# 28 identity matmuls on TensorE ahead of the transposes behind a double norm

## The reference

```python
# end of the first block, last layer
x = layer_norm(ALPHA * x + 0.5 * swiglu(x, ffn_w_gu[l, 1], ffn_w_down[l, 1]), ln_g[l, 2], ln_b[l, 2])
...
# start of the second block
h = rms_norm(x, norm1_g[l])
z = h @ w_in[l]
```

## Time and profile before

| | us |
|---|---|
| median of 3 runs | 1911.38 |
| lowest and highest run | 1909.96, 1911.92 |
| the profiled execution's own time | 1909.5 |
| its span, first to last instruction | 1907.7 |
| TensorE busy in it | 1878.9 |
| VectorE busy | 1259.6 |
| ScalarE busy | 968.5 |
| TensorE waiting between 950 and 1000 us | 5.0 |

### The profile page before, as it was taken

The page is one execution under the profiler, slowest core; times in us unless marked ns, Lnnn a source line. Parts: engine busy times, 40 slices in busy tenths (PEclk is TensorE's granted clock), DMA queues, the critical chain, the costliest instruction groups (busy, mean ns, idle before and its releaser), DMA issues.

```text
span 1907.7 us, 26911 instructions
## 1 busy us (share of the span) xinstructions
PE 1878.9 (98%) x10465; PEld 1633.4 (86%) x10465; DVE 1259.6 (66%) x1598; ACT 968.5 (51%) x1242; POOL 35.8 (2%) x67
## 2 busy tenths in 40 slices
PE   9999989999999999999989999999999999999998
PEld 7888877888888888788879988889989998889987
DVE  4465876456646678745576887676556787776554
ACT  5454664454455456545446445555544645554543
POOL 1010100000000000000000000000000000000000
PEclk9999999999999999999999999999999999999999
DMA  9666535655665564566546554466565554355562
GB/s 321 194 193 220 195 105 189 196 178 186 206 192 183 182 183 146 178 204 184 186 142 197 168 174 133 138 204 180 186 196 177 183 188 155 122 182 174 185 194 81
DMA packets 173580, 342.52 MB, mean 180 GB/s; under 512 B 10976, under 2 KB 11152, under 8 KB 173344
## 3 DMA queue, kind: packets, MB, share of 16 engines
q1 hardware_dynamic: 169360, 327.26, 54.5%
q0 software_dynamic: 4112, 13.77, 2.1%
HBM read 338.36 MB, written 1.05 MB: 178 GB/s over the span
## 4 chain that ended last, share of the span: by engine, by line
PE 91%; DVE 6%; ACT 2%; issue 1%; DMA 0%; SPq 0%; DVEq 0%; ACTq 0%
PE stream L2203 18%; PE stream L2205 18%; PE stream L2204 18%; PE stream L2370 7%; PE stream L2372 7%; PE stream L2371 7%; PE aux L2250 2%; PE aux L2612 1%; PE stream L2241 1%; DVE wlo L1242 1%; PE stream L2232 1%; PE stream L2233 1%; PE stream L2309 1%; PE stream L2311 1%; PE stream L2310 1%; PE aux L2671 1%
## 5 line engine op out<-in xcount | busy, mean ns | idle before, releaser
L1242 DVE TENSOR_TENSOR wlo<-raw,whi 128x1024 fp32r<-128x1024 f32 x584 | 708.2, 1223 | 540.7 <-ACT whi L717 537.9
L717 ACT ACTIVATE whi<-raw 128x1024 fp32r<-128x1024 f32 x584 | 612.3, 1057 | 615.5 <-PE stream L2205 431.9
L2203 PE MATMUL stream<-whi,xhi 128*128 128x512 f32 x944 | 372.6, 395 | 2.1 <-DVE wlo L1242 2.0
L2205 PE MATMUL stream<-whi,xlo 128*128 128x512 f32 x944 | 368.1, 390 | 0.0
L2204 PE MATMUL stream<-wlo,xhi 128*128 128x512 f32 x944 | 367.5, 389 | 0.0
L2370 PE MATMUL stream<-xhi,whi 128*128 128x256 f32 x1184 | 336.9, 285 | 0.0
L2372 PE MATMUL stream<-xhi,wlo 128*128 128x256 f32 x1184 | 335.0, 283 | 0.0
L2371 PE MATMUL stream<-xlo,whi 128*128 128x256 f32 x1184 | 335.0, 283 | 0.0
L2203 PE MATMUL stream<-whi,hhi 128*128 128x512 f32 x672 | 263.3, 392 | 0.0
L2205 PE MATMUL stream<-whi,hlo 128*128 128x512 f32 x672 | 261.6, 389 | 0.0
L2204 PE MATMUL stream<-wlo,hhi 128*128 128x512 f32 x672 | 261.5, 389 | 0.0
(11 more groups left out here) (334 smaller groups left out, 1751.4 us busy)
## 6 DMA issues: line engine op xcount, KB each, us to landing
raw<-ffn_w_gu SPq DMA_DIRECT2D x176, 512.0 KB, 4.4
raw<-w_in SPq DMA_DIRECT2D x136, 512.0 KB, 4.6
raw<-ffn_w_down SPq DMA_DIRECT2D x88, 512.0 KB, 3.7
raw<-w_up SPq DMA_DIRECT2D x64, 512.0 KB, 4.1
raw<-w_down SPq DMA_DIRECT2D x64, 512.0 KB, 4.1
raw<-c_w_in SPq DMA_DIRECT2D x24, 512.0 KB, 4.0
raw<-ab_w_in SPq DMA_DIRECT2D x20, 512.0 KB, 5.2
raw<-w_out SPq DMA_DIRECT2D x16, 512.0 KB, 3.6
```

The source lines that it names most:

```text
L717: act.activation(split_slots(lin, at, j)[0], raw[:, b % RAW], ACT.Copy).then_inc(hi_ready, 1)
L1242: dve.tensor_tensor(lo, raw[:, b % RAW], hi.bitcast(F32), ALU.subtract).then_inc(lo_ready, 1)
L2203: pe.matmul(bank[tt][:], hi, wh, start=kt == 0, stop=False)
L2205: mm = pe.matmul(bank[tt][:], lo, wh, start=False, stop=kt == last)
```

## The change

A function `fill(n)` is added to TensorE's program. It waits until the next auxiliary bank is free and multiplies the identity table by itself `n` times into its first 128 columns. It gives no signal and takes no bank: the transposes that follow write over the same bank. It is called with 28 in the one stage with two norms, between the last matmul of the down projection and the transposes of token tile 0.

```diff
+            def fill(n):
+
+                pe.wait_ge(aux_free, seen.aux - AUX + 1)
+                for _ in range(n):
+                    pe.matmul(aux[seen.aux % AUX][:, 0:P], ident, ident, start=True, stop=True)
+
             def turn(src, first, n, more=0):
...
                 rows(lin, At(1), xh, xl, tail=tail)
                 if len(st.norms) == 2:
+                    fill(28)
                     x_turn(src, 0, 0)
                 x_turn(src, 0, 1)
```

## The result

| | before | with the 28 matmuls |
|---|---|---|
| median of 20 runs, us | 1910.58 | 1914.45 |
| lowest and highest | 1909.84, 1911.92 | 1912.47, 1915.35 |
| profiled execution, its span | 1909.5, 1907.7 | 1912.98, 1911.2 |

The ratio is 1.0017 with a 95% interval of 1.0011 to 1.0023: 3.2 us more, between 2.1 and 4.4. The medians alone lie 3.9 us apart. The forecast was 3.2 us more. The change makes the kernel slower by about a sixth of a per cent.

A forecast was written before the change was run, and what follows sets the result against it. TensorE bounds most of the kernel, but VectorE's chain holds the double norm; 1.7 (overrun) + 0 (kept clock) + 1.5 (second gap) = 3.2 us, so 1911.4 + 3.2 = 1914.6 us, range 1912.2 to 1917.0.

The forecast's parts named there:

- The place: Double norm, 973 to 992 us: VectorE holds the chain, so the 2.6 us TensorE loses in tile 0 is hidden.
- The fill's length: Before tile 0's transposes: 28 matmuls are 56 passes of 0.107 us, 6.0 us, upper end 6.3.
- The overrun: Fill ends 2.2 us after tile 0 is ready; VectorE's chain slips by 1.7 us, 2.0 at the upper pass price.
- The kept clock in tile 0: Tile 0 at full clock saves TensorE 2.6 us, but nothing waits for it: 0 on the path.
- The second gap: TensorE's idle time before tile 1 grows from 1.17 to 2.8 us; clock loss costs 0 to 3.0, taken as 1.5.
- The clock holds: Rival: clock stays full through the gap before tile 1, only the overrun costs, 1913.1 us; chance 0.30.
- The fill fits: Rival: 28 one-pass matmuls take 3.1 us, end before tile 0 is ready, time stays 1911.4 us; chance 0.11.
- Faster: Rival: TensorE's catching up in tile 0 sets tile 1, kept clock gives up to 2.6 us, 1908.8; chance 0.04.

The follow-up runs named there:

- e2: Kernel before plus 17 identity matmuls before tile 0's transposes and 14 before tile 1's; 1911.33 us against 1911.17, ratio 0.9998.
- e5: Changed kernel with 42 identity matmuls instead of 28; 1916.22 us against 1911.21 for the kernel before, ratio 1.0027.
- e1: Changed kernel with 17 identity matmuls instead of 28; 1913.68 us against 1911.17 for the kernel before, ratio 1.0012.
- e7: Kernel before, no fill, second half of the second norm's last scaling moved from VectorE to ScalarE; 1911.38 us against 1911.21, ratio 1.0003.
- e4: Changed kernel with its 28 fill matmuls replaced by 28 transposes of the identity table; 1914.02 us against 1911.17 for the kernel before, ratio 1.0012.
- e6: Changed kernel with 8 identity matmuls instead of 28, run once; stage 22.94 us against 21.34 for the kernel before.
- e8: Kernel before plus 17 and 14 fill matmuls before tiles 0 and 1, and half a scaling moved to ScalarE; 1910.71 us against 1911.21, ratio 0.9993.
- e3: Changed kernel, its 28 matmuls kept, plus 11 before tile 1's transposes; 1913.34 us against 1911.17 for the kernel before, ratio 1.0006.
- e9: Kernel before with fills of 8 and 4 matmuls in the attention mixer, none at the double norm; 1911.01 us against 1911.07, ratio 0.9998.

## Why the prediction was right

- **The place.** That VectorE holds the chain between 973 and 992 us, and that TensorE's slow tile 0 is hidden, was read from the chain and from the 1.17 us of idle time. e2 shows it for the profiled executions: full clock throughout, the same stage to 0.01 us.
- **The fill's length.** Predicted 56 passes of 0.107 us, 6.0 us, upper end 0.112 and 6.3; measured 56 of 0.111, 6.24. The lower price came from dividing the distance to the next instruction by 16; the steps between the records themselves gave the better figure.
- **The overrun.** Predicted 1.7 us on VectorE's chain (2.0 with the upper price); measured 1.95, and 3.13 more for 14 more matmuls (e5). The 0.25 us too little is all in the price of a pass.
- **The kept clock in tile 0.** Value put at 0; measured 0 in e1 and e2. The forecast said that nothing waits for TensorE's catching up; e7 adds that this holds only as long as VectorE is no faster.
- **The second gap.** Predicted 2.8 us of idle time, measured 2.88. The cost of the clock there was the open term, 0 to 3.0 with 1.5 taken; measured 1.23 in the profile and 1.2 to 2.4 in the other kernels with a gap of 2.9 to 3.3 us. The reason given for a lower value, a shorter slow stretch, is what the rows show: 3.4 us at half clock against 6.8 before. The place of the fall was not as assumed. The upper end had it 2.2 us into the gap and 0.6 us before work resumes; it came 3.3 us after the gap began (991.8 to 995.1), half a microsecond into tile 1's transposes. The 1.5 was the middle of two ends, not a cost worked out, and that it lies close to 1.23 is luck.
- **The rivals.** "The clock holds" (0.30) did not occur in any of the five profiles with a gap of 2.88 us or more (the change, e1, e4, e5, e6). "The fill fits" fell with the 56 records; where it was made to fit (e1, e4), the time did not stay at before's, as that rival had it. It had overlooked that a fill which fits gives the second gap 3.3 us and loses the clock there. "Faster" fell with e1 and e2, whose tile 1 came no earlier and whose medians are not lower, and with it the price that the Trainium skill's rule (section Terms of the page on the clock gate) gives for throttled time: the rule counts TensorE's time, not the kernel's, and the 6.8 us at half clock, 3.4 by that rule, cost the stage nothing.

The sum came out as 1.95 + 1.23 = 3.18 us in the stage, against 1.7 + 1.5 = 3.2: two errors of a quarter of a microsecond that cancel. The forecast of 1914.6 us also meets the median of 1914.45 by a second cancelling: it started from 1911.38, the median of three runs, 0.8 us above the 1910.58 of the 20, and the medians moved by 3.9 us in place of 3.2. And the prediction took about 0.2% as the least that can be told from no change; the interval here is 0.06% to either side, and 0.17% stands clear of it.

## What to carry to other kernels

Before filling a gap to keep TensorE's clock, look whether TensorE is idle again a little later: if it is, the slow stretch is paid out of that idle time, and keeping the clock only makes the second gap longer, and behind that one the clock can fall with nothing to hide it. Count a fill in passes as the trace records them (a plain f32 matmul is two), and check it against the time from the last instruction's issue slot to the release, since every pass beyond delays whoever waits for the next result. Where two engines arrive level at a hand-over, neither a faster one nor the other gains anything by itself (e2, e7); only both together do (e8).

## What the runs showed of the hardware

- The clock's fall is not decided by the length of a gap alone. Around the same gap of 1.84 us at 272 it stayed at 1.00 before and fell in e2, e3 and e5, 1 to 1.6 us after the gap; it fell behind one of 2.1 us in e9, and stayed through 1.8 us in e6. When it fell ahead of tile 1, work ran at half clock for 3.4 us (the change, e1, e5, e6) or for most of 6.8 (e4), at a price of 1.2 to 2.4 us. It does not always fall inside the gap: in the change it fell 0.5 us after TensorE had gone back to work, in e5 0.7 us and in e6 1.9 us, but in the kernel before 2.2 us into the gap.
- This makes part of the scatter. In e2 the stage began 2.2 us later than in the kernel before, with its stage of the same length.
- An f32 128x128 matmul is two records of 0.111 us each; a transpose of the same tile is one, 28 of them in 3.2 us, and 28 transposes kept the clock as 17 matmuls did.
